# A two-layer block on one core: the token mixer in two parts, and layer 1's first mixer inside layer 0's last expert tile

## The chip, the cores and the metric

The kernel runs on one core of a Trainium2 chip, in fp32. The metric is the device time in microseconds (us) of one execution. The engines of the core work side by side and meet at semaphores: TensorE (PE: matrix products and transposes into PSUM), VectorE (DVE), ScalarE (ACT), GpSimd (POOL: here it issues the gathers) and SyncE (SP: here it issues the weight loads). Each engine goes through its own instructions strictly in order. All transfers share 16 DMA engines.

## The reference

Two layers act on 4 tiles of 128 latent tokens and 2 tiles of 128 context tokens, width 1024. Each layer has a token mixer and then a PEER expert layer, each followed by a residual and a layer norm:

```python
y, y_x = token_mixer(modulate(x, sh1, sc1), modulate(ctx, xsh1, xsc1), ...)
x = layer_norm(alpha * x + g1 * y, ln1_g[layer], ln1_b[layer])
f = peer(modulate(x, sh2, sc2), w_pq[layer], sub_keys[layer], u_tab[layer], v_tab[layer])
x = layer_norm(alpha * x + g2 * f, ...)      # and the same for ctx in layer 0
```

The mixer projects its input with w_in and forms three branches. Branch a is dense grouped attention with RMS norm and rope (8 heads, 2 key heads) over all 6 tiles; branch c is attention over a window of 128 tokens to either side, plus the context, with a sink; branch b is a convolution of three taps over the tokens, `gb * conv(gc * xb)`. Then `m = sum(sigmoid(gate_i) * (y_i @ w_branch[i]))` and `m @ w_out`. In layer 1 the context gives keys and values alone.

PEER picks for each token and each of 8 heads 16 of 16384 experts (product keys), gathers a row of u_tab and one of v_tab for each, 1024 wide, and returns `sum(gelu(x . u) * softmax * v)`.

## The kernel before

**Order.** `ORDER` names ten (layer, tile) units: 0 and 1 are layer 0's context tiles, 2 to 5 its latent tiles, 6 to 9 layer 1's latent tiles. Unit n is first mixed (mixer n) and then goes through its expert tile n. An expert tile has 128 slots. In slot S POOL issues one gather of u (128 partitions by 1024 fp32, one expert for each token) and one gather of v for 36 slots earlier (`BEHIND`); DVE forms the dot product of a u row (line 1463); PE sums two v rows in every second slot (`two_sums`), into banks 0 and 1 of PSUM. Both rings, ur and vr, hold 6 rows. A new u gather waits for the dot of the row six back, a v gather for the sum of the row six back. Every 16 slots a head is routed (top 16, on DVE), and PE makes the query product of a head three ahead, with two chunks of w_pq.

**The plan.** `plan()` (line 95) writes one list of steps, and all engines go through the same list. An entry is a slot (l, S) with the steps that it hosts, or steps alone. `hosted(n)` (line 123) says what expert tile n hosts:

- every tile n that is not the last of its layer hosts mixer n + 1, in 83 steps, one a slot from slot 0, and `turn` at slot 83. A mixer's step `mix(m, at)`: at 0 to 40 attention, eight pairs of heads, five slots a pair (scores, maxima, exponentials, transposes, copy; values and transposes of the pair before go in between), the dense branch first; 41 to 70 the merge, six groups (two halves of 512 columns by three branches) of four gate chunks and two branch chunks; 72 to 75 eight chunks of w_out; 76 to 82 residual and norm;
- tile 0 hosts beside that, from slot 87 and two a slot, the projections of both latent pairs of layer 0 (`proj` 1 and 2), their convolution over 512 columns (`conv` 1) and a row;
- tile 5, which hosts no mixer, has the 12 modulation pieces of layer 1 (48 chunks), five rows, the keys of the context (`proj` 3) and keys and queries of tiles 0 and 1 (`proj` 4).

Then layer 0 runs out: 36 slots of v rows, the end of tile 5 (`ends`), and then alone, with no slots beside it: `proj` 5 (keys and queries of tiles 2 and 3, which needs the new x of unit 5), `conv` 2 over 512 columns, mixer 6 in 83 steps, `turn`, and the lead (product, routing of the first heads). I call this stretch the seam. A similar stretch with mixer 0 opens the kernel.

**Data.** A `proj` job turns x tiles, modulates them into xTg (8 x 512 columns per partition), takes keys and values (`kT`, `vals`), queries, and spills turned x (xts), queries (qts) and convolution results (yts) to DRAM. A mixer loads its tile's qTt, xTt and ybt back. xTg and the mixer's buffers lie in one arena and overlap. hn, the input of the dot products, is made by `tile_begins` (lines 1453 and 1455) on DVE from x and two broadcast rows. Twenty such rows (`row`) are made by transposes and an ACT copy.

**Weights.** All weights come in chunks of 128 x 1024 fp32 (512 KB) over a ring of five, in the order of the plan (`load`, line 396); SP stops at the sixth until `w_used` says that the first was used. On line 399 stands

```python
w.wait_ge("w_used", c - NS + 1)
sp.dma_start(wring[:, c % NS, :], src).then_inc(w_in[c % NS], 16)
```

PE's hosted work uses banks 4 to 7; banks 0 to 3 belong to the experts.

Of the kernel before, what the change touches and what calls it, by code (L numbers as in the profile page):

```python
# [17 lines left out]
P = 128  # L18
D = 1024
# [5 lines left out]
HD = 64  # L25
# [45 lines left out]
def row_source(r):  # L71

    return {R_G1: (True, G1), R_S2: (True, SC2), R_H2: (True, SH2), R_G2: (True, G2),
            R_L1G: (False, 0), R_L1B: (False, 1), R_L2G: (False, 2), R_L2B: (False, 3)}[r]
# [3 lines left out]
ROWS = ([(r, 0, 1) for r in (R_G1, R_L1G, R_L1B, R_S2, R_H2, R_G2, R_L2G, R_L2B)]  # L78
        + [(R_G1, 0, 0), (R_S2, 0, 0), (R_H2, 0, 0), (R_G2, 0, 0)]
        + [(r, 1, 0) for r in (R_G1, R_L1G, R_L1B, R_S2, R_H2, R_G2, R_L2G, R_L2B)])  # L80


def rows_for_mix(m):
    return 8 if m < 2 else 9 if m < 6 else 17


def rows_for_h(n):
    return 8 if n < 2 else 11 if n < 6 else 17


def rows_for_end(n):
    return 8 if n < 2 else 12 if n < 6 else 20


def plan():


    out = []
    for e in range(4):
        out.append((None, [("mod", e, 0)]))  # L100
        if e:
            out.append((None, [("mod", e - 1, 1)]))
    out.append((None, [("mod", 3, 1)]))
    out += [(None, [("proj", 0, st)]) for st in range(18)]
    out += [(None, [("conv", 0, st)]) for st in range(16)]

    def begin(m, beside):
        for s in range(83):
            out.append((None, [("mix", m, s)] + beside.get(s, [])))
        out.append((None, [("turn", m)]))  # L110
        l = ORDER[m][0]
        for jj, st in ((0, 0), (0, 1), (0, 2), (1, 0), (0, 3), (1, 1), (1, 2), (0, 4), (2, 0), (1, 3), (2, 1), (2, 2), (1, 4)):
            out.append((None, [("lead", l, jj, st)]))

    beside = {}
    for e in range(4, MODS):
        beside.setdefault(4 * (e - 4) + 1, []).append(("mod", e, 0))
        beside.setdefault(4 * (e - 4) + 3, []).append(("mod", e, 1))
    for r in range(8):
        beside.setdefault(33 + r, []).append(("row", r))  # L120
    begin(0, beside)

    def hosted(n):
        at = {}
        if n + 1 < FIRST[ORDER[n][0]] + COUNT[ORDER[n][0]]:
            for s in range(83):
                at[s] = [("mix", n + 1, s)]
            at[83] = [("turn", n + 1)]
        if n == 0:
            steps = ([("proj", 1, st) for st in range(18)] + [("proj", 2, st) for st in range(18)]  # L130
                     + [("conv", 1, st) for st in range(16)] + [("row", 8)])
            for i, step in enumerate(steps):
                at.setdefault(87 + i // 2, []).append(step)
        elif n == 1:
            at[100], at[102] = [("row", 9)], [("row", 10)]
        elif n == 2:
            at[100] = [("row", 11)]
        elif n == 5:
            for e in range(MODS):
                at.setdefault(4 + 3 * e, []).append(("mod", MODS + e, 0))  # L140
                at.setdefault(6 + 3 * e, []).append(("mod", MODS + e, 1))
            for r in range(12, 17):
                at.setdefault(44 + 2 * (r - 12), []).append(("row", r))
            for i, st in enumerate((0, 1, 2, 3, 4, 5, 6, 7, 8, 9, 10)):
                at.setdefault(56 + i, []).append(("proj", 3, st))
            for st in range(18):
                at.setdefault(70 + 2 * st, []).append(("proj", 4, st))
        elif n == 6:
            at[100], at[102], at[104] = [("row", 17)], [("row", 18)], [("row", 19)]
        return at  # L150

    for l in range(LAYERS):
# [11 lines left out]
def chunk_counts(steps):  # L164

    used, n = {}, 0
    for at, beside in steps:
# [7 lines left out]
        for d in beside:  # L175
            if d[0] == "mod" and d[2] == 0:
                n += 4
            elif d[0] == "proj" and (2 <= d[2] < 6 or PAIRS[d[1]][3] and (6 <= d[2] < 10 or 11 <= d[2] < 15)):
                n += 1
            elif d[0] == "conv" and d[2] % 4 < 3:  # L180
                n += 1
            elif d[0] == "mix" and 41 <= d[2] < 71:
                n += len(CHUNKS_AT[(d[2] - 41) % 5])
# [35 lines left out]
def hybrid_dit_peer(nc, x, ctx, cc, w_mod, b_mod, w_qkv, q_norm, k_norm, conv_w, sink, w_conv, w_gb,  # L219
                    w_out, ln, w_pq, sub_keys, u_tab, v_tab, rope_c, rope_s, out):  # L220
    with ExitStack() as stack:
# [125 lines left out]
        def far_scores():  # L347

            return bank(5).rearrange("p (h n) -> p h n", h=2)
# [1357 lines left out]
```

## Time and profile before

| | before |
|---|---|
| median of 3 runs | 5172.78 us (5172.71 to 5173.66) |
| the profiled execution | 5177.72 us |
| its span | 5176.0 us |
| PE, DVE, POOL busy | 3824.4, 2791.6, 2779.3 us |
| moved by DMA | 1796.82 MB, mean 347 GB/s |
| granted clock of TensorE, mean | 0.86 |

The engines' names in the rows are as above; PEld is the weight load of TensorE, SPq a transfer's issue. `x8` counts instructions; an fp32 product with 512 columns counts as two. A row of a window has its stretch, its length, the busy times of PE, PEld, DVE, ACT and POOL with the count of instructions, then the granted clock, the DMA share and GB/s. The windows inside tiles begin and end at the dot product of a slot that 16 divides. The granted clock is a share of 2.4 GHz. The DMA share is the mean busy share of the 16 engines. Expert tiles n began (hn written) at 348.7 (0), 894.7, 1316.6, 1738.9, 2166.6, 2582.3 (5), 3487.7 (6), 3915.0, 4341.5 and 4761.1 us (9).

### The profile page before, as it was taken

To read this page: it belongs to the slowest core of one execution; us is meant where nothing else is said; L and a number is where in the kernel's file an instruction comes from. 1 tells how busy PE (TensorE), PEld (TensorE's weight loads), DVE (VectorE), ACT (ScalarE), POOL (GpSimd) and SP (SyncE) were. 2 spreads that over 40 slices of the span, in tenths; PEclk is the share of its full clock that TensorE was granted. 3 is DMA by queue.
4 is the path that set the end of the run, shared out by engine and by line. 5 is a ranking of instruction groups with operands and counts; after the bars stand their busy time and mean duration, and the time that the engine had idled before them with its cause. 6 is when DMAs were issued, how large, how long until landed. Compare 5 with 4: busy or idle time off the path is not lost.

```text
span 5176.0 us, 47460 instructions
## 1 busy us (share of the span) xinstructions
PE 3824.4 (74%) x15312; PEld 1709.4 (33%) x15312; DVE 2791.6 (54%) x7071; ACT 866.8 (17%) x1954; POOL 2779.3 (54%) x2575
## 2 busy tenths in 40 slices
PE   7767788885886787688666759587867866876555
PEld 4543333431432342243223214445323323421111
DVE  1156454746755665675645622126467556656662
ACT  1211111311311221131101100213112212210100
POOL 0026523756756765775755640004567557657775
PEclk9878899998998898899778989586989988998787
DMA  6679976999999999999999972066999999999998
GB/s 209 220 265 369 402 261 241 372 409 408 391 388 408 391 379 406 395 384 409 407 409 392 404 282 87 33 245 211 408 406 384 382 410 399 381 409 407 399 408 314
DMA packets 509655, 1796.82 MB, mean 347 GB/s; under 512 B 56288, under 2 KB 71904, under 8 KB 509152
## 3 DMA queue, kind: packets, MB, share of 16 engines
q0 software_dynamic: 368640, 1342.34, 66.8%
q1 hardware_dynamic: 122336, 438.34, 22.2%
q10 hardware_dynamic: 18432, 13.11, 0.8%
q8 instruction: 123, 2.02, 0.2%
q14 instruction: 124, 1.02, 0.1%
HBM read 1778.36 MB, written 15.20 MB: 347 GB/s over the span
## 4 chain that ended last, share of the span: by engine, by line
DMA 38%; PE 36%; issue 10%; POOL 7%; DVE 6%; ACT 2%; SPq 0%; POOLq 0%; DVEq 0%
PE ps L568 33%; DMA vr<-in_v_tab,idxT 30%; DMA ur<-in_u_tab,idx 5%; POOL ur L530 4%; POOL vr L541 3%; PE ps L571 3%; DMA wring<-in_w_mod 2%; DVE ur L1463 1%; DVE mx L1357 1%; ACT arena L1064 1%; DVE mx L1355 1%; ACT arena L983 1%; ACT arena L1067 0%; DMA wring<-in_w_out 0%; DVE ps L1352 0%
## 5 line engine op out<-in xcount | busy, mean ns | idle before, releaser
L568 PE MATMUL ps<-vr,spread 128*32 128x512 f32 x5120 | 1526.0, 727 | 975.1 <-DMA vr<-in_v_tab,idxT 926.8
L1463 DVE CUSTOM_DVE_ANT_0 ur<-ur,hn 128x1024 f32<-128x1024 f32 x1280 | 1564.3, 1222 | 1183.2 <-DMA ur<-in_u_tab,idx 1180.3
L530 POOL DMA_INDIRECT ur<-in_u_tab,idx x1280 | 1383.3, 1081 | 1273.2 <-DVE idx L1546 742.9
L541 POOL DMA_INDIRECT vr<-in_v_tab,idxT x1280 | 1392.3, 1088 | 1103.6 <-PE ps L568 492.4
L568 PE MATMUL ps<-wring,arena 128*128 128x512 f32 x2272 | 1042.0, 607 | 13.6 <-ACT arena L983 9.4
L568 PEld LDWEIGHTS ps<-vr,spread 128*32 128x32 f32 x5120 | 312.1, 122 | 1869.4 <-issue 1865.4
L568 PEld LDWEIGHTS ps<-wring,arena 128*128 128x128 f32 x2272 | 426.0, 194 | 550.7 <-issue 522.9
L568 PE MATMUL ps<-wring,hT 128*128 128x256 f32 x1280 | 339.5, 413 | 7.4 <-ACT hT L983 6.0
L571 PE MATMUL ps<-ident,arena 128*128 128x128 f32 x1000 | 188.2, 334 | 188.1 <-DVE arena L1381 103.2
L568 PEld LDWEIGHTS ps<-wring,hT 128*128 128x128 f32 x1280 | 251.1, 206 | 157.2 <-issue 115.5
L571 PEld LDWEIGHTS ps<-ident,arena 128*128 128x128 f32 x1000 | 144.5, 170 | 282.5 <-DVE arena L1381 140.7
L568 PE MATMUL ps<-vals,arena 128*128 128x64 f32 x1472 | 208.6, 304 | 22.7 <-ACT arena L1082 17.4
L568 PEld LDWEIGHTS ps<-vals,arena 128*128 128x128 f32 x1472 | 201.5, 219 | 54.4 <-ACT arena L1082 32.6
L568 PE MATMUL ps<-arena,wring 128*128 128x512 f32 (+1 forms) x576 | 212.4, 531 | 3.8 <-issue 3.8
L1108 ACT COPY q_sb<-ps 128x256 f32<-128x256 f32 x80 | 29.8, 373 | 952.4 <-PE ps L568 952.4
L568 PE MATMUL ps<-kT,arena 64*128 64x256 f32 (+2 forms) x576 | 144.2, 557 | 13.4 <-DMA arena<-qts 13.4
L568 PEld LDWEIGHTS ps<-arena,wring 128*128 128x128 f32 x576 | 111.7, 195 | 101.9 <-issue 96.3
L1064 ACT ACTIVATE arena<-ps,nm 128x512 f32<-128x512 f32 (+2 forms) x160 | 91.7, 573 | 221.9 <-DVE nm L1368 221.9
L568 PE MATMUL ps<-wring,csilu 128*32 128x128 f32 x1536 | 80.3, 350 | 53.2 <-DMA wring<-in_w_mod 53.0
L1355 DVE TENSOR_REDUCE mx<-ps 128x2 f32<-128x512 f32 x64 | 43.8, 684 | 139.0 <-PE ps L568 139.0
L1089 ACT ACTIVATE arena<-ps 128x512 f32<-128x512 f32 x60 | 35.8, 597 | 487.4 <-PE ps L568 487.0
L1463 DVE DVE_READ_ACCUMULATOR2_ANT dots<- 128x1 f32 x1280 | 105.8, 83 | 0.0
(158 smaller groups left out, 2686.3 us busy)
## 6 DMA issues: line engine op xcount, KB each, us to landing
wring<-in_w_gb SPq DMA_DIRECT2D x360, 512.0 KB, 7.8
wring<-in_w_pq SPq DMA_DIRECT2D x160, 512.0 KB, 8.0
wring<-in_w_mod SPq DMA_DIRECT2D x96, 512.0 KB, 7.2
wring<-in_w_out SPq DMA_DIRECT2D x80, 512.0 KB, 7.6
wring<-in_w_qkv SPq DMA_DIRECT2D x64, 512.0 KB, 6.7
ur<-in_u_tab,idx POOLq DMA_INDIRECT x1280, 8.2
vr<-in_v_tab,idxT POOLq DMA_INDIRECT x1280, 8.3
wring<-in_w_conv SPq DMA_DIRECT2D x36, 512.0 KB, 3.6
```

The costliest lines, as they stand in the source:

```text
L530: nc.gpsimd.indirect_dma_start(ur[:, row % UR, :], None, u_rows, bass.IndirectOffsetOnAxis(ap=idx[:, at:at + 1], axis=0)).then_inc(u_in[ro ...
L541: nc.gpsimd.indirect_dma_start(vr[:, row % VR, :], None, v_rows, bass.IndirectOffsetOnAxis(ap=idxT[:, pair % 3, i:i + 1], axis=0)).then_in ...
L568: return nc.tensor.matmul(o, lhsT, rhs, start=first, stop=last, skip_group_check=True)
L571: return nc.tensor.transpose(o, src, ident[:])
L983: m = nc.scalar.activation(o[:, k, :], bank(b + k // 4, k % 4 * P, (k % 4 + 1) * P), ACT.Identity, scale=mod_t[:, l, KD * scale + k, kind: ...
L1064: k = nc.scalar.activation(pr[:, hd, 0:n], bank(4 + 2 * hd, 0, n), ACT.Exp, bias=bias, scale=SCALE, accum_out=sums[:, a % 2, 0, hd:hd + 1])
L1089: nc.scalar.activation(sg, bank(4 + 2 * (e6 % 2)), ACT.Sigmoid).then_inc(s["sg_done"], 1)
L1108: nc.scalar.copy(flat(q_sb), bank(2, 0, 2 * P)).then_inc(s["q_copied"], 1)
L1355: ch.inc(v.tensor_reduce(mx[:, a % 2, 1, :], far_scores(), AX, ALU.max))
L1357: ch.inc(v.tensor_reduce(top2, near_scores(0, n), AX, ALU.max))
L1463: v.tensor_tensor_reduce(u, u, hn[:], 1.0, 0.0, ALU.mult, ALU.add, dots[:, j % 2, k:k + 1]).then_inc(s["dots_done"], 1)
```

## The change

The single numbered jobs are split into small steps, and the plan puts groups of them into slots. In particular:

- `proj` becomes keys jobs (two tiles or one; the last, LATE, is tile 3 of layer 1 alone) and queries jobs (two tiles). Queries and convolutions of tiles 2 and 3 are moved into a later expert tile; xTg is read back from xts for them. A convolution job now covers two tiles with one column of overlap (258 columns), five jobs in place of three.
- A mixer is two parts: windowed attention, then the merge of the convolution branch, of the windowed branch and of the dense branch's gates; then dense attention, then the merge of the dense branch (`merge_last`), w_out, norm. For mixer 6 the first part is hosted in tile 5, and the second stands alone after the last tile's keys, with two dense pairs in work at a time: the second in PSUM banks 0 to 3 and in the u buffers.
- The modulation pieces of layer 1 move from tile 5 to tile 4. The rows R_S2 and R_H2 go (20 rows become 14); hn is now made by PE, which turns hT back at slot 127 of the tile before, and a DVE copy.
- A mixer's loads on SP wait until every chunk issued so far was used, and for all spills so far.

```diff
+KEYS = [(0, (4, 5)), (0, (0, 1)), (0, (2, 3)), (1, (4, 5)), (1, (0, 1)), (1, (2,)), (1, (3,))]
+LATE = 6
+QUERIES = [(0, 4, False), (0, 0, False), (0, 2, True), (1, 0, False), (1, 2, True)]
+CONVS = [(0, 4, 0, 256, 0), (0, 0, 0, 258, 0), (0, 2, 254, 258, 2), (1, 0, 0, 258, 0), (1, 2, 254, 258, 2)]
+BRANCHES = (1, 2, 0)
+GROUP_CHUNKS = ((0, 1, 2, 3, 4, 5), (0, 1, 2, 3, 4, 5), (0, 1, 2, 3)) * 2 + ((4, 5), (4, 5))
...
+def keys_job(j):
+    tiles = KEYS[j][1]
+    return ([[("xt", j, i)] for i in range(len(tiles))] + [[("kvp", j, part)] for part in range(4)] + [[("kvv", j)]]
+            + [[("kvr", j, i)] for i in range(len(tiles))] + [[("kvt", j)]])
+def queries_job(j):
+    return ([[("qx", j)]] + [[("qp", j, 0, part)] for part in range(4)] + [[("qs", j), ("qp", j, 1, 0)]]
+            + [[("qr", j, 0, 0), ("qp", j, 1, 1)], [("qr", j, 0, 1), ("qp", j, 1, 2)], [("qp", j, 1, 3)], [("qt", j, 0)]]
+            + [[("qr", j, 1, 0)], [("qr", j, 1, 1)], [("qt", j, 1)]])
+def attention(m, br):
+    qs = range(4) if br else range(4, 8)
+    out = [[] for _ in range(24)]
+    for i, q in enumerate(qs):
+        for off, kind in enumerate(("sc", "mx", "ex", "tp", "ev", "va", "yn", "ty", "yc")):
+            out[5 * i + off].append((kind, m, q))
+    return out
+def attention_alone(m):
+    order = ("sc4 sc5 mx4 ex4 mx5 ex5 tp4 ev4 sc6 mx6 va4 yn4 tp5 ev5 ex6 ty4 yc4 sc7 mx7 va5 yn5 tp6 ev6 ex7 ty5 yc5 "
+             "va6 yn6 tp7 ev7 ty6 yc6 va7 yn7 ty7 yc7").split()
...
+def merge_last(m):
+    out = [[("gp", m, 6, 4)], [("gp", m, 6, 5)], [("gp", m, 7, 4), ("ml", m, 6)], [("gp", m, 7, 5)], [("mt", m, 0), ("ml", m, 7)]]
+    out += [[("wo", m, 0)], [("wo", m, 1)], [("mt", m, 1), ("wo", m, 2)]] + [[("wo", m, k)] for k in range(3, KD)]
+    return out + [[("on", m, st)] for st in range(7)]
...
+    def mixer(m):
+        return [[("in", m)]] + attention(m, 1) + merge_first(m) + attention(m, 0) + merge_last(m)
...
+        if n == 0:
+            put(mixer(1), 0, 73)
+            put([[("turn", 1)], [("row", 6)]], 74, 76)
+            put(keys_job(1) + keys_job(2), 76, 104)
+            put(queries_job(1), 104, 126)
+        elif n == 1:
+            put(conv_job(1), 0, 18)
+            put(mixer(2), 18, 85)
+            put([[("turn", 2)]], 85, 86)
+            put(queries_job(2) + conv_job(2), 87, 126)
+        elif n in (2, 3, 7, 8):
+            put(mixer(n + 1), 0, 84)
+            put([[("turn", n + 1)]], 84, 85)
+            if n == 2:
+                put([[("row", 7)]], 100, 101)
+        elif n == 4:
+            put(mixer(5), 0, 78)
+            put([[("turn", 5)]], 78, 79)
+            put([[("mod", MODS + e, 0)] + ([("mod", MODS + e - 1, 1)] if e else []) for e in range(MODS)]
+                + [[("mod", 2 * MODS - 1, 1)]], 80, 126)
+        elif n == 5:
+            put([[("row", 8)], [("row", 9)], [("row", 10)]] + keys_job(3) + keys_job(4), 0, 28)
+            put(queries_job(3), 28, 42)
+            put(keys_job(5), 43, 53)
+            put(conv_job(3), 53, 72)
+            put([[("in", SPLIT)]] + attention(SPLIT, 1) + merge_first(SPLIT), 72, 128)
+        elif n == 6:
+            put(mixer(7), 0, 84)
+            put([[("turn", 7)]], 84, 85)
+            put([[("row", 11)], [("row", 12)], [("row", 13)]] + queries_job(4) + conv_job(4), 86, 126)
         if n + 1 < FIRST[ORDER[n][0]] + COUNT[ORDER[n][0]]:
+            put([[("hn", n + 1)]], 127, 128)
...
         if l == 0:
-            out += [(None, [("proj", 5, st)]) for st in range(18)]
-            out += [(None, [("conv", 2, st)]) for st in range(16)]
-            begin(6, {})
+            alone(keys_job(LATE) + attention_alone(SPLIT) + merge_last(SPLIT))
+            lead(SPLIT)
...
+                elif kind == "in":
+                    if c["kv"]:
+                        w.wait_ge("w_used", ring[0])
+                    for k in range(c["kv"]):
+                        if kept(k):
+                            w.wait_ge(f"xsp{k}", 16 * len(KEYS[k][1]))
+                    for k in range(c["q"]):
+                        w.wait_ge(f"qsp{k}", 32)
+                    for k in range(c["cv"]):
+                        w.wait_ge(f"ysp{k}", 64)
+                    w.wait_ge("y_read", c["out"])
...
+            def turn_back(n):
+                free_banks(("hn", n))
+                w.wait_ge("hT_done", n + 1)
+                for k in range(KD):
+                    m = turn(bank(4 + k // 4, k % 4 * P, (k % 4 + 1) * P), hT[:, k, :])
+                m.then_inc(s["hn_mm"], 1)
...
             def tile_begins(n):
-                ch.inc(v.tensor_tensor(hn[:], xt, rows[:, R_S2, :], ALU.mult))
-                ch.wait()
-                v.tensor_tensor(hn[:], hn[:], rows[:, R_H2, :], ALU.add).then_inc(s["hn_done"], 1)
+                w.wait_ge("hn_mm", n + 1)
+                v.tensor_copy(hn[:], ps[:, 4 * BW:6 * BW]).then_inc(s["hn_done"], 1)
```

`put(groups, lo, hi)` spreads the groups evenly over the slots lo to hi. `free_banks(d)` lets PE wait, at the first product of a job, until all jobs that the plan has before it have left their banks.

## Rows read from the trace of the kernel before

**Rows 1.** Page, 40 slices: busy share of the DMA engines, tenths
```profile
DMA  6679976999999999999999972066999999999998
```

**Rows 2.** Windows by stage: us, busy per engine, clock, DMA share, GB/s
```profile
349.00:895.00 546.00, 435.20 (x1376) 194.35 (x1378) 299.49 (x751) 87.98 (x194) 246.96 (x220) 0.87 0.85 315
...
895.00:1317.00 422.00, 319.79 (x1274) 137.62 (x1272) 265.51 (x681) 83.72 (x189) 279.53 (x258) 0.89 1.01 397
...
1739.00:2167.00 428.00, 323.85 (x1282) 138.81 (x1280) 268.30 (x686) 84.34 (x187) 278.89 (x258) 0.88 1.00 391
...
2582.00:3016.00 434.00, 293.28 (x1690) 117.56 (x1690) 241.40 (x592) 56.60 (x114) 267.31 (x253) 0.83 1.02 402
...
3078.00:3242.00 164.00, 136.77 (x326) 62.63 (x324) 42.59 (x75) 13.30 (x29) 0.00 (x0) 0.89 0.27 84
...
3242.00:3366.00 124.00, 78.06 (x310) 61.58 (x311) 21.10 (x59) 30.00 (x95) 0.00 (x0) 0.53 0.07 27
...
3366.00:3447.00 81.00, 79.39 (x188) 35.11 (x187) 7.18 (x11) 7.58 (x11) 0.00 (x0) 0.97 0.79 275
...
3447.00:3488.00 41.00, 22.82 (x90) 16.86 (x90) 25.00 (x87) 8.30 (x23) 5.62 (x6) 0.75 0.54 194
...
3488.00:3915.00 427.00, 307.93 (x1130) 152.01 (x1132) 257.99 (x669) 80.91 (x183) 246.12 (x220) 0.81 0.90 346
...
4761.00:5099.00 338.00, 198.04 (x686) 56.21 (x683) 217.37 (x523) 27.20 (x50) 256.92 (x253) 0.79 1.02 404
```

**Rows 3.** Windows inside tile 0 (two) and tile 5 (one), 16 slots each
```profile
381.00:415.00 34.00, 18.13 (x73) 13.28 (x73) 31.45 (x94) 11.65 (x33) 22.68 (x18) 0.60 0.87 291
...
689.00:848.00 159.00, 149.06 (x420) 65.88 (x421) 59.93 (x138) 19.61 (x39) 32.39 (x33) 0.95 0.65 213
...
2647.00:2717.00 70.00, 40.93 (x413) 18.95 (x407) 27.31 (x76) 4.04 (x11) 35.57 (x32) 0.74 1.03 409
```

**Rows 4.** TensorE's timeline, seam: start, us, what [idle before <-releaser]
```profile
3086.37 1.94 PE L571 MATMUL ps<-ident,x_all 128*128 128x128 f32 x8 [8.23 <-DVE x_all L1595]
...
3096.26 30.06 PE L568 MATMUL ps<-wring,arena 128*128 128x512 f32 x64 [2.99 <-ACT arena L983]
...
3150.08 85.37 PE L568 MATMUL ps<-arena,wring 128*128 128x512 f32 x192 [1.15 <-issue]
...
3242.69 3.36 PE L568 MATMUL ps<-kT,arena 64*128 64x512 f32 x8 [7.23 <-DMA arena<-qts]
...
3260.61 3.37 PE L568 MATMUL ps<-kT,arena 64*128 64x512 f32 x8
...
3268.81 2.82 PE L571 MATMUL ps<-ident,arena 128*128 128x128 f32 x12 [1.33 <-ACT arena L1067]
...
3273.22 3.74 PE L568 MATMUL ps<-vals,arena 128*128 128x64 f32 x24 [1.59 <-ACT arena L1082]
...
3311.14 2.51 PE L568 MATMUL ps<-kT,arena 64*128 64x256 f32 x8
...
3460.14 6.70 PE L568 MATMUL ps<-wring,hT 128*128 128x256 f32 x16 [2.99 <-ACT hT L983]
```

**Rows 5.** Timeline of all engines: a key chain's ends, and hn of tile 6
```profile
3112.63 0.65 ACT L1008 COPY vals<-ps 128x256 f32<-128x256 f32 x2 [16.42 <-PE ps L568]
...
3119.16 0.42 DVE L1231 TENSOR_TENSOR arena<-ps,arena 128x256 f32<-128x256 f32 x1
...
3487.65 1.22 DVE L1453 TENSOR_TENSOR hn<-x_all,rows 128x1024 f32<-128x1024 f32 x1
```

**Rows 6.** Window over the first 48 slots of tile 2
```profile
1319.00:1466.00 147.00, 124.64 (x652) 66.72 (x649) 112.71 (x298) 47.86 (x124) 109.14 (x96) 0.93 0.97 374
```

**Rows 7.** Timeline of TensorE: one query chunk in tile 2
```profile
1341.56 1.89 PE L568 MATMUL ps<-wring,hT 128*128 128x256 f32 x8
```

**Rows 8.** DMA issues: count, KB each, median us from issue to landing
```profile
arena<-qts SPq DMA_DIRECT2D x10, 512.0 KB, 6.9
...
ur<-in_u_tab,idx POOLq DMA_INDIRECT x1280, 8.2
```

More of the change, by code:

```diff
@@ L99, in plan @@
     for e in range(4):
-        out.append((None, [("mod", e, 0)]))
+        alone([[("mod", e, 0)]])
         if e:
[L102 to L111, printed above, removed]
+            alone([[("mod", e - 1, 1)]])
@@ L116, in plan @@
+    groups = mixer(0)
     for e in range(4, MODS):
[L117 to L121, printed above, removed]
+        groups[4 * (e - 4) + 1].append(("mod", e, 0))
+        groups[4 * (e - 4) + 3].append(("mod", e, 1))
+    for r in range(EARLY_ROWS):
+        groups[40 + 2 * r].append(("row", r))
+    alone(groups)
@@ L123, in hosted @@
+    lead(0)
     def hosted(n):
         at = {}
-        if n + 1 < FIRST[ORDER[n][0]] + COUNT[ORDER[n][0]]:
[L126 to L149, printed above, removed]
@@ new lines, in values @@
+            def values(m, q):
+                a = 8 * m + q
+                br, _, at = pair_of(m, q)
+                near, far = keys_of(m, br)
+                tiles = near + far
+                w.wait_ge("pts_done", a + 1)
+                w.wait_ge("yT_done", a - (1 if two_at_a_time(m, q) else 0))
+                for half in range(2):
+                    for b, kt in enumerate(tiles):
+                        k = mm(bank(7 - 4 * at, half * HD, (half + 1) * HD), pts[at][:, half, b, :],
+                               vals[:, br, kt, half * HD:(half + 1) * HD], b == 0, b == len(tiles) - 1)
+                k.then_inc(s["pv_mm"], 1)
@@ L1035, in conv, with turned @@
-            def conv(g, st):
-                l, t0, nt = GROUPS[g]
+            def turned(j, i):
+                l, tiles = KEYS[j]
+                w.wait_ge("tx_mm", XT_BEFORE[j] + i + 1)
+                for before in range(j):
+                    if kept(before):
+                        w.wait_ge(f"xsp{before}", 16 * len(KEYS[before][1]))
+                o = columns(j, i)
+                modulate(o, 4, l, int(tiles[i] >= LAT), SH1, SC1).then_inc(s["xT_done"], 1)
+                if kept(j):
+                    act.wait_ge(s["xT_done"], XT_BEFORE[j] + i + 1)
+                    nc.scalar.dma_start(xts[l, tiles[i]], o).then_inc(s[f"xsp{j}"], 16)
@@ new lines, in values_out @@
+            def values_out(j):
+                w.wait_ge("w_used", USED["kvp", j, 3])
+                tiles = KEYS[j][1]
+                n = len(tiles)
+                for i in range(n):
+                    m = nc.scalar.copy(vals[:, :, tiles[i], :], bank(6 + i, 2 * P, BW).rearrange("p (a b) -> p a b", b=P))
+                m.then_inc(s["v_copied"], 1)
+                w.wait_ge("ksq_done", j + 1)
+                nc.scalar.activation(kss[:, 0:n, :], kss[:, 0:n, :], ACT.Sqrt).then_inc(s["ksd_done"], 1)
```

1212 lines of the change are left out of this document (614 added, 598 removed).

## The prediction

> **What bounds the kernel now.** I read the slices of the page first [rows 1]: the DMA engines stand at 9 tenths or more in 29 of 40 slices; the holes are the first slices, 6 and 7, and 24 to 28. Then the windows by stage [rows 2]. A slot below is one of the 128 steps of an expert tile. Each window of an expert tile runs from one tile's hn to the next. Tiles 1 to 5, 7 and 8 have a DMA share of 1.00 to 1.02 at 391 (tile 3) to 402 GB/s (tile 5); 1, 3 and 5 are shown. They take as long as their bytes, 415 to 434 us. Tile 9, which hosts nothing, takes 338. Three stages are not DMA bound. Tile 0 takes 546 us at 315 GB/s, and most of that excess is in one stretch [rows 3]: 16 slots take 159 us there, TensorE is busy 149 of them. The seam between the layers (3078 to 3488) takes 410 us at 27 to 275 GB/s, with POOL idle. Tile 6 has 346 GB/s, as its first 36 slots have no v gathers beside them. Last I followed the seam on TensorE [rows 4]: transposes and keys and queries of the last two tiles, a convolution over 512 columns (192 instructions, 85.37 us), attention, merge, norm, lead.
>
> So the question is what the seam loses, and what the hosting tiles pay.
>
> **The seam.** What stays in it after 3078, where its last v sum ends:
> - Norm of x, 8.2 us (the idle before the transposes), then one tile's transposes and modulation, 1.94 + 2.99: 13.1 us, against 18.2 before for two tiles [rows 4].
> - Four key chunks for one tile. 64 instructions took 30.06 us [rows 4], so 16 take 7.5. The key chain that lay under the query product is now bare: on two tiles it ran from the v copy at 3112.63 to the rope's end at 3119.58 [rows 5], 7.0 us; I take 5 for one, plus 1.3 for transposes and copy: 13.8.
> - Four dense pairs of heads. Alone they took 68 us, from the first scores at 3242.69 to those of the next branch at 3311.14 [rows 4], 17.1 each. Of the pair shown TensorE worked 3.37 (scores) + 0.47 (y, estimated from one of eight at the lower clock) + 2.82 (transposes) + 3.74 (values) = 10.4 us; the rest is waiting for maxima and exponentials. With two pairs in two sets of banks the work of one covers the waits of the other. Walking the written order with these durations (the first two pairs' scores, maxima and exponentials to 8.4; 11 to 12 for each later pair; the last one's waits bare) I get 54 us. Ends: 34 (TensorE's share halved, were it at the upper clock) and 68 (no overlap).
> - Four branch chunks and eight of the out projection, 16 and 32 instructions at 0.44 (85.37 / 192 [rows 4]), 21; products with the gates, adds and row transposes between, 2.6 by similar rows: 23.6.
> - Norm, transposes, modulation up to the first query as at the seam's start, 13.1. Then hT is turned back for hn, 8 transposes, 2.0 by the 1.94 of such a row. Lead 27.5 as before (3460.14 [rows 4] to hn at 3487.65 [rows 5]).
>
> Sum 13.1 + 13.8 + 54 + 23.6 + 13.1 + 2.0 + 27.5 = 147 us against 410: **-262 us**, ends -285 and -235.
>
> A rule weighs here. The granted clock of the attention window of the seam was 0.53, near the 1.2 GHz level, while the merge after it ran at 0.97 [rows 2]; TensorE worked there in bursts of 3 to 4 us with waits of 1.3 and 1.6 between them [rows 4]. The Trainium skill (TensorE: Matmul & The Clock Gate, "HAM oscillation — how this bites in real kernels") says that short bursts with idle gaps bring the array back to the lower clock each time. The trace agrees with that for one pair at a time. By the page, closing the gaps with a second pair could release the clock; the attention would then come to the 34 us end above. I keep the lower level, since waits are left in the walk.
>
> **What tiles pay.** In a DMA-bound tile 1 MB more costs 2.5 us (402 GB/s), a chunk (0.524 MB) 1.3 us.
> - *Tile 0*: 80 hosted chunks become 60, less spill of queries and yts: 172 MB (315 x 546) to 159. At 400 GB/s that is 399; slots 16 to 31 ran at 291 GB/s for 34 us [rows 3], the 16 before them much the same, so 64 us with 18 lost; 8 for stalls. 425, **-121** (ends -146 and -86: key steps sit 1.4 slots apart).
> - *Tile 1*: gets both convolutions of layer 0 (24 chunks), the late queries (8) and the reload of three xts tiles. 167.5 MB becomes 189: 470 us by bytes. TensorE: 320 busy now [rows 2], plus 2 x 46 for the convolutions (192 instructions each, 8 of 256 columns in 1.89 us [rows 7]), 32 for queries, 4 for rows and hn: 448. In a mixer's first 48 slots, which hold its eight pairs, it idled 22 of 147 us [rows 6], and 102 of 422 in all. The mixer is also squeezed from 83 slots into 67, a pair every 3.3 slots. I take 510, **+88** (ends +48 and +140).
> - *Tiles 2, 3, 7, 8*: same bytes. A pair comes every 4.2 slots rather than 5; eight pairs took about 122 us (40 of the 48 slots in 147 us [rows 6]), 15.2 each; 4.2 slots would take 11 at tile 9's 2.64 us a slot (338 / 128). The chain, not the slot, sets this, and attention now drains twice: **+4 each, +16** (ends -10, +60).
> - *Tile 4*: takes over 48 modulation chunks, 25.2 MB: +63, and +4 as above: **+67** (ends +60, +90). These chunks already ran at 409 GB/s in tile 5 [rows 3].
> - *Tile 5*: 64 chunks before (48 + 4 + 12), 64 after (12 keys, 8 queries, 12 convolution, 32 merge). Bytes no change. New: SP waits before the mixer's loads until every issued chunk is used and the last spill of the convolution has landed; behind it stand the merge's weights, and TensorE waits for q. A q load took 6.9 us to land [rows 8]; with the spill ahead and two slots between, 8 net. The convolution needs 46 us of TensorE in 19 slots: 9 over bytes. Two chained stretches: 9. **+26** (ends 0, +66).
> - *Tile 6*: 20 chunks, reload and spills, 14 MB: 35, and 5 of stalls: **+40** (ends +30, +70).
> - *hn*: VectorE no longer makes hn with two passes (1.22 each [rows 5]) but copies out of PSUM, 1.2 as one such pass, after TensorE has done the last two-row sum (1.9) and 8 transposes (2.0). That v row is issued behind the last u row on POOL, so the first dot comes some 4 us later. Five u rows are in flight meanwhile and landing takes 8.2 us [rows 8], so I charge 1 us in 8 tiles: **+8** (ends -5, +30).
> - *Prologue*: two rows fewer, one hn more, attention in two parts; **-2**.
>
> Sum: -262 - 121 + 88 + 16 + 67 + 26 + 40 + 8 - 2 = **-140 us**. The profiled execution took 5177.7 us (span 5176.0), so 5038; the median of the runs is 4.9 us lower: **5033 us**.
>
> Cross-check by idle DMA time. Added are 24 convolution chunks, 4 of keys and 6 reloads, 34 x 0.524 = 17.8 MB, 44 us. The seam's 410 us carried 47 MB (its four windows [rows 2]), 118 us at 402, so 292 idle; after it carries 13 MB in 147 us, 115 idle. Tile 0 had 116 idle and keeps 26. That is 44 - 177 - 90 = -223 with no new stall anywhere, the most there is: 4950.
>
> **Rivals.**
> 1. *Everything hides* (0.09): the tiles run at 400 GB/s also with the new work, and most of the 80 us between the two sums is not there: 4965 with 15 left, 4950 with none. For it: TensorE has room, 320 of 422. Against: it works in order and idles in each attention chain.
> 2. *Half is given back* (0.20): tiles 0, 1 and 6, with keys, queries and convolution at a step per 1.1 to 1.4 slots, come near their upper ends together (35 + 52 + 30 of 117): 5105 to 5160. Tile 0 before is its evidence: 16 slots in 159 us with two steps a slot [rows 3]. Against: half the columns and half the density now.
> 3. *Slower* (0.06): the period of a hosted pair. If putting its steps into 4.2 slots makes each pair slower, since TensorE stands in the chain while v gathers wait (a ring of six), sixty pairs in tiles 1 to 8 pay. From 15.2 us a pair, 140/60 = 2.3 more, so 17.5, wipes the gain out; at 19 (the seam's 17.1 with one two-row sum of 1.9 between) it is +228 - 140 = +88: 5261. Against it: hosted pairs ran at 0.93 of the clock, not 0.53 [rows 2, 6].
> 4. *The seam doesn't shrink as written* (0.02 of its own, no change in all): TensorE's waits for all earlier stages, or the bare key chain, would have to cost 140 more than the 147: 5173.
>
> **How the numbers follow.** The forecast has 0.63: its own range by adding the ends as independent, about 70 either way. The range 4960 to 5115 takes that in, with part of rivals 1 and 2. Differences under 0.2% (10 us) can't be told from none here. Faster 0.90, same 0.03, slower 0.07.
>
> **What would show it.** From the last v sum of layer 0 to hn of tile 6: 147 us, the dense attention 54 of it, two sets of scores back to back. Tile 0 near 425, tile 1 near 510 with TensorE busy about 450, tile 4 near 483 at 400 GB/s, tile 5 near 460, tile 6 near 467, tiles 2 and 3 within 10 of before. It is wrong if the seam is over 200, or if the DMA share of tiles 2, 3, 7, 8 falls clearly under 0.98.

## The result, and the profile after

| | before | after | ratio, 95% interval |
|---|---|---|---|
| median | 5173.22 us | 4993.77 us | 0.9645, 0.9623 to 0.9667 |
| span of the profiled execution | 5176.0 | 4985.6 | |

The kernel is 3.6% faster, 179 us at the medians and 190 in the profiled spans. Forecast were 140 and 5033 us; the range 4960 to 5115 holds the time.

The windows by stage of the changed kernel, to be read against [rows 2]; they run from one tile's hn to the next. The row of 61 us is the run-out of layer 0's v rows, the row of 145 us the seam, and the last one tile 6:

```profile
0.00:370.00 370.00, 278.81 (x1554) 169.04 (x1554) 68.04 (x195) 56.56 (x139) 9.56 (x21) 0.85 0.58 205
370.00:784.00 414.00, 324.33 (x1128) 138.21 (x1128) 268.76 (x702) 82.40 (x187) 253.06 (x225) 0.90 1.01 394
784.00:1281.00 497.00, 421.85 (x1728) 221.87 (x1728) 293.32 (x750) 87.29 (x197) 284.94 (x252) 0.92 0.97 371
1281.00:1714.00 433.00, 329.53 (x1296) 141.25 (x1296) 266.44 (x683) 84.02 (x186) 282.80 (x261) 0.88 1.01 393
...
2143.00:2625.00 482.00, 352.92 (x2046) 162.83 (x2047) 264.26 (x693) 84.35 (x197) 284.14 (x255) 0.88 1.01 399
2625.00:3076.00 451.00, 363.37 (x1368) 161.69 (x1366) 260.96 (x647) 75.52 (x172) 275.07 (x251) 0.92 1.00 387
3076.00:3137.00 61.00, 40.08 (x152) 9.53 (x148) 1.59 (x5) 3.38 (x4) 29.95 (x32) 0.89 0.88 313
3137.00:3282.00 145.00, 95.53 (x354) 63.52 (x352) 50.05 (x140) 31.96 (x83) 5.62 (x6) 0.75 0.27 94
3282.00:3726.00 444.00, 366.25 (x1432) 192.10 (x1432) 279.47 (x718) 87.99 (x193) 253.40 (x222) 0.89 0.95 365
```

The seam fell from 410 to 145 us. Tile 0 went from 315 to 394 GB/s: it is now bound by its bytes like the others, and 132 us shorter. Tile 4 still moves 399 GB/s and is 66 us longer, which is what 48 chunks cost. Of the expert tiles only tile 1 (0.97, with TensorE busy 422 of 497 us) and tile 6 (0.95) have a DMA share below 1.00. The profile's page says the same of the whole; against [rows 1] only slices 1 to 3 and 26 to 27 are still holes:

```profile
DMA  5749999999999999999999999359999999999998
```

By stages, from the first dot of one tile to the first dot of the next (the seam: from the end of the last v sum to the first dot):

| stage | before | after | difference | forecast |
|---|---|---|---|---|
| up to the first dot | 351.2 | 370.1 | +19 | -2 |
| tile 0 | 546.0 | 414.1 | -132 | -121 |
| tile 1 | 421.9 | 496.6 | +75 | +88 |
| tiles 2, 3, 7, 8 | 1696.0 | 1715.2 | +19 | +16 |
| tile 4 | 415.7 | 481.5 | +66 | +67 |
| tile 5 with the run-out | 493.3 | 515.2 | +22 | +26 |
| seam | 412.0 | 142.3 | -270 | -262 |
| tile 6 | 427.4 | 443.3 | +16 | +40 |
| tile 9 and the end | 412.4 | 407.4 | -5 | 0 |
| hn (in the tiles above) | | | | +8 |

The seam on TensorE, changed kernel, to be read against [rows 4]:

```profile
3148.09 1.97 PE L686 MATMUL ps<-ident,x_all 128*128 128x128 f32 x8 [8.14 <-DVE x_all L1741]
3153.05 9.78 PE L683 MATMUL ps<-wring,arena 128*128 128x512 f32 x16 [2.99 <-ACT arena L1099]
3167.07 0.69 PE L686 MATMUL ps<-ident,arena 128*128 128x128 f32 x2 [4.25 <-DVE arena L1381]
3168.22 5.29 PE L683 MATMUL ps<-kT,arena 64*128 64x512 f32 x16 [0.46 <-ACT kT L1131]
...
3189.37 2.77 PE L686 MATMUL ps<-ident,ur 128*128 128x128 f32 x12
3191.93 0.42 PE L686 MATMUL ps<-ident,arena 128*128 128x128 f32 x1
3193.72 1.89 PE L683 MATMUL ps<-kT,arena 64*128 64x512 f32 x8 [1.38 <-ACT ur L1204]
3195.55 2.89 PE L683 MATMUL ps<-vals,ur 128*128 128x64 f32 x24
...
3216.26 8.90 PE L683 MATMUL ps<-wring,arena 128*128 128x512 f32 x16 [0.35 <-ACT arena L1210]
3253.98 1.97 PE L686 MATMUL ps<-ident,hT 128*128 128x128 f32 x8 [2.99 <-ACT hT L1099]
```

Two pairs' scores stand together as `x16`; from there to the end of the last y transposes, 3168.22 to 3215.91, it is 47.7 us where the walk gave 54 and one pair at a time took 68 in the kernel before. The bare key chain is the 4.25 us of idle before 3167.07. Part of the reason for 47.7 rather than 54 is the clock: scores took 5.29 for the first two pairs and 1.89 for the last, where the walk had 3.37 each. The window over the stretch has the granted clock at 0.64 and TensorE busy for 38.4 us, where the walk had 41.6. The waits are the other half, 9.3 us against 12.4 (54 less 41.6).

```profile
3168.00:3216.00 48.00, 38.44 (x180) 31.71 (x180) 10.96 (x28) 17.12 (x46) 0.00 (x0) 0.64 0.00 1
```

### The profile page after: what moved, and what is told of

It is laid out like the page before. It is cut to its first block, busy times and chain, and to the rows that moved or that the text cites. A ratio compares the mean times of both kernels' runs of the same rounds, so it can differ in the third digit from the quotient of the medians.

```text
span 4985.6 us, 48540 instructions
## 1 busy us (share of the span) xinstructions
PE 3777.8 (76%) x15728; PEld 1743.7 (35%) x15728; DVE 2774.0 (56%) x7108; ACT 867.4 (17%) x1963; POOL 2799.3 (56%) x2575
## 2 busy tenths in 40 slices
DMA packets 519164, 1814.71 MB, mean 364 GB/s; under 512 B 56961, under 2 KB 77697, under 8 KB 518657
## 4 chain that ended last, share of the span: by engine, by line
PE 38%; DMA 37%; issue 9%; DVE 7%; POOL 6%; ACT 3%; SPq 1%; POOLq 0%; ACTq 0%; DVEq 0%
PE ps L683 34%; DMA vr<-in_v_tab,idxT 27%; DMA ur<-in_u_tab,idx 5%; POOL ur L645 3%; PE ps L686 3%; POOL vr L656 3%; DMA wring<-in_w_gb 2%; DVE ur L1609 1%; DMA wring<-in_w_mod 1%; ACT arena L1187 1%; DVE mx L1500 1%; DMA wring<-in_w_pq 1%; ACT arena L1099 1%; ACT arena L1190 1%; DMA wring<-in_w_qkv 1%
## 5 line engine op out<-in xcount | busy, mean ns | idle before, releaser
L683 PE MATMUL ps<-vr,spread 128*32 128x512 f32 x5120 | 1477.1, 705 | 764.7 <-DMA vr<-in_v_tab,idxT 728.6
L645 POOL DMA_INDIRECT ur<-in_u_tab,idx x1280 | 1399.7, 1093 | 1020.4 <-DVE idx L1692 494.6
L683 PE MATMUL ps<-wring,arena 128*128 128x512 f32 x2272 | 1078.5, 619 | 51.4 <-DMA wring<-in_w_gb 21.5
L683 PE MATMUL ps<-wring,hT 128*128 128x256 f32 x1280 | 323.8, 398 | 22.2 <-DMA wring<-in_w_pq 22.2
L683 PE MATMUL ps<-arena,wring 128*128 128x258 f32 (+1 forms) x960 | 218.1, 385 | 4.8 <-ACT arena L1151 3.5
L683 PEld LDWEIGHTS ps<-vals,arena 128*128 128x128 f32 x1424 | 185.5, 211 | 58.3 <-ACT arena L1204 33.8
L683 PEld LDWEIGHTS ps<-arena,wring 128*128 128x128 f32 x960 | 181.3, 191 | 44.3 <-issue 13.4
L683 PE MATMUL ps<-kT,arena 64*128 64x256 f32 (+2 forms) x576 | 144.3, 558 | 53.1 <-DMA arena<-qts 36.5
L1526 DVE TENSOR_TENSOR arena<-ps,rec 128x128 f32<-128x128 f32 x80 | 23.3, 292 | 202.8 <-PE ps L683 202.2
L1187 ACT ACTIVATE arena<-ps,nm 128x256 f32<-128x256 f32 (+2 forms) x156 | 88.8, 570 | 218.0 <-DVE nm L1511 218.0
L683 PEld LDWEIGHTS ps<-kT,arena 64*128 64x128 f32 x576 | 79.2, 220 | 98.4 <-issue 47.0
```

The lines of the kernel that those rows point to most:

```text
L645: nc.gpsimd.indirect_dma_start(ur[:, row % UR, :], None, u_rows, bass.IndirectOffsetOnAxis(ap=idx[:, at:at + 1], axis=0)).then_inc(u_in[ro ...
L683: return nc.tensor.matmul(o, lhsT, rhs, start=first, stop=last, skip_group_check=True)
L1187: k = nc.scalar.activation(pr[at][:, hd, 0:n], bank(b + 2 * hd, 0, n), ACT.Exp, bias=bias, scale=SCALE, accum_out=sums[:, a % 2, 0, hd:hd ...
L1526: v.tensor_tensor(ysb[:, a % 2, :].rearrange("p (h f) -> p h f", f=HD), bank(7 - 4 * at, 0, P).rearrange("p (h f) -> p h f", f=HD), over(r ...
```

## The experiments

They ran in three groups, and in each the kernel before took longer than above: 5329 us in the first group (mixer 6 not split, one pair at a time, steps spread, hT at slot 125 for the first time), 5354 and 5353 in the other two. So a whole time is compared inside its group, by its ratio to the kernel before. The first group had no run of the changed kernel; for stages I take it from the others. Four experiments were executed once each (mixer 6 not split, one pair at a time, steps spread, attention first), and they are read by their stages. A stage that an edit doesn't touch still differs by 5 to 10 us between runs, so a single pair of stages shows no less than that.

**Mixer 6 not split.**

```diff
-            put([[("in", SPLIT)]] + attention(SPLIT, 1) + merge_first(SPLIT), 72, 128)
...
-            alone(keys_job(LATE) + attention_alone(SPLIT) + merge_last(SPLIT))
+            alone(keys_job(LATE) + [[("in", SPLIT)]] + attention(SPLIT, 1) + merge_first(SPLIT)
+                  + attention_alone(SPLIT) + merge_last(SPLIT))
```

> Mixer 6 is not split: tile 5 hosts keys, queries and convolution only, and windowed attention and the first merge of mixer 6 stand alone in the seam. Theory A (a hosting tile pays for bytes): tile 5 gets shorter by 32 chunks at 1.3 us, 42, and by some 10 us of waits for the mixer's loads, 50 in all; the seam gets longer by four windowed pairs at 13.8 us, 55, by 32 chunks at 4 x 0.44 us, 56, and a load of about 8: 118. Sum +68 against the changed kernel, about 5055 profiled. Rival B (tile 5 has TensorE time to spare and hosts the part nearly for nothing): tile 5 shorter by under 15, sum over +100. Rival C (most of the seam's gain came from the moved convolution and queries, the split is worth little): sum under +30.

Tile 5 with its hosted work gone, and the seam:

```profile
2664.00:3078.00 414.00, 305.68 (x1104) 125.80 (x1104) 247.10 (x609) 54.94 (x112) 274.41 (x250) 0.85 0.98 378
3141.00:3393.00 252.00, 179.93 (x610) 110.44 (x605) 64.94 (x178) 52.37 (x143) 5.64 (x6) 0.76 0.36 128
```

The seam is 251 us from the last v sum to the first dot, 109 more than the changed kernel's 142 (expected 118). From first to last dot tile 5 takes 415 us against 461 and 468 in the two runs of the same group that hosted the part: 46 to 53 less (expected 50). So hosting pays some 50 us for 109. The whole took 5172 us, 0.9706 of before, against 0.9586 and 0.9598 for the changed kernel: 1.1% or about 60 us, where theory A expected 68, rival B over 100 and rival C under 30. Theory A holds. Convolution and queries moved out, keys of one tile, and the dense pairs two at a time brought the seam from 412 to 251, some 160 of the 270 us; the split brought the rest. Of the 160, only the pairs were tested by themselves, in the next experiment.

**One pair at a time in the seam.**

```diff
-            alone(keys_job(LATE) + attention_alone(SPLIT) + merge_last(SPLIT))
+            alone(keys_job(LATE) + attention(SPLIT, 0) + merge_last(SPLIT))
```

> The four dense pairs in the seam one after the other instead of two at a time. Theory (the second pair covers the waits of the first): the stretch from the first dense scores to the end, 48 us in the changed kernel, goes back to 68 or a little less, +18 to +20, granted clock back from 0.66 towards 0.53. Rival (TensorE's own work at the lower clock sets it): under +6.

Its timeline on TensorE, one pair and the next pair's scores:

```profile
3233.04 3.21 PE L683 MATMUL ps<-kT,arena 64*128 64x512 f32 x8
3236.18 0.33 PE L686 MATMUL ps<-ident,arena 128*128 128x128 f32 x1
3241.08 2.82 PE L686 MATMUL ps<-ident,ur 128*128 128x128 f32 x12 [4.57 <-ACT ur L1190]
3245.49 5.38 PE L683 MATMUL ps<-vals,ur 128*128 128x64 f32 x24 [1.59 <-ACT ur L1204]
3250.80 3.37 PE L683 MATMUL ps<-kT,arena 64*128 64x512 f32 x8
```

The window over the four pairs, to be read against that of 48 us above:

```profile
3215.00:3286.00 71.00, 45.46 (x181) 35.84 (x182) 11.45 (x28) 17.45 (x45) 0.00 (x0) 0.55 0.00 0
```

A pair takes 17.8 us, with waits of 4.57 and 1.59. The seam from last v sum to first dot is 166 us against 142, +24, a little over the +18 to +20 expected. From the first scores to the last y transpose it is 70.4 us against 47.7, 22.7 more. Of these 7 are TensorE's own work (45.5 us busy against 38.4, at a granted clock of 0.55 against 0.64) and the other 16 are waits. So the second pair gains twice: it fills waits, and for part of the time the products run at the upper clock. The rival, under 6 us, is out.

**Tile 0's steps spread, in the kernel before.**

```diff
-                at.setdefault(87 + i // 2, []).append(step)
+                at.setdefault(87 + i * 39 // 53, []).append(step)
```

> The kernel before, with the 53 steps that tile 0 hosts after its mixer (projections, convolution over 512 columns, a row) over slots 87 to 126 instead of 87 to 113. Theory A (TensorE's work was the limit there: 149 of 159 us busy): tile 0 shorter by some 15 to 25 us only, because 13 more slots of gathers lie beside the same work, 546 to about 525. Rival B (two steps a slot, each waiting for another engine, made the stall): shorter by 60 or more.

The hosted steps now lie over both windows (the first dot of slot 80 to that of 96, and from there to the end):

```profile
683.00:776.00 93.00, 78.29 (x261) 34.43 (x259) 53.99 (x131) 16.30 (x33) 33.07 (x31) 0.93 0.84 299
776.00:885.00 109.00, 104.91 (x290) 45.12 (x292) 40.79 (x91) 7.21 (x13) 27.54 (x27) 0.97 0.60 197
```

Tile 0 is 8 us shorter than in [rows 2], in a run whose tile 1 is 12 longer for a reason that lies outside the edit. The gain is 8 us as measured and about 20 if tile 0 was slowed as tile 1 was. The changed kernel's tile 0 took 0 to 6 us more in these groups than above, so the truth is more likely near 10: under theory A's 15 to 25, and far from the 60 of rival B. TensorE is busy 105 of 109 us in the second window, as it was 149 of 159 in [rows 3]. So the density of the steps was not the matter. That it was the amount of products is argued from these busy times: the changed kernel, which has the convolution elsewhere, keeps TensorE busy 324 us in tile 0 against 435.

**hT turned back at slot 125.**

```diff
-            put([[("hn", n + 1)]], 127, 128)
+            put([[("hn", n + 1)]], 125, 126)
```

> hT is turned back for hn at slot 125 instead of slot 127. In the changed kernel the first dot of a tile came 8 to 9 us after the last dot before it in tiles 1, 3, 4, 8 (4.1 before the change). Theory A (the wait for TensorE's last two-row sum is exposed and costs DMA time): that gap falls to 3 to 4 us in all tiles, and the time by 3 us in each of 5 tiles, 10 to 20 in all. Rival B (the DMA queues stay full through the gap, as the prediction had it with 1 us a tile): the gap falls but the time by under 6.

> hT turned back at slot 125, now beside the changed kernel on one chip. The gap before a tile's first dot, summed over the eight tile starts within a layer, was 52 us in the changed kernel and 35 with this edit. Theory A (exposed): 10 to 17 us less time. Rival B (hidden by the gathers in flight): under 5.

What it was to cure is this, in the changed kernel at the start of tile 4 (the last dot of tile 3, TensorE's last two-row sum, the transposes, the copy, the next dot):

```profile
2134.49 1.23 DVE L1609 CUSTOM_DVE_ANT_0 ur<-ur,hn 128x1024 f32<-128x1024 f32 x1 [3.08 <-DMA ur<-in_u_tab,idx]
2137.15 3.63 PE L683 MATMUL ps<-vr,spread 128*32 128x512 f32 x8 [5.44 <-DMA vr<-in_v_tab,idxT]
2140.71 1.33 PE L686 MATMUL ps<-ident,hT 128*128 128x128 f32 x8
2142.07 1.22 DVE L1601 COPY hn<-ps 128x1024 f32<-128x1024 f32 x1 [5.93 <-PE ps L686]
2143.33 1.23 DVE L1609 CUSTOM_DVE_ANT_0 ur<-ur,hn 128x1024 f32<-128x1024 f32 x1
```

The gap between two dots is 8.8 us here. With the edit the eight gaps summed to 35 us in the first group and 32 in the other instead of 52, as expected, but the time did not follow. Beside the changed kernel the ratios were 0.9597 (0.9575 to 0.9619) with the edit and 0.9598 (0.9573 to 0.9622) without, in the first group 0.9588 with it. That favours rival B, but each interval is some 12 us to either side, so 10 us can't be ruled out by this pair. Nor is it shown that the gathers in flight bridge the gap: tile 5 with the run-out took 531 to 543 us in the four runs with this edit and 521 to 533 in six without it, for a cause that stays open, and that alone may hide a gain.

**The modulation pieces under the second attention of mixer 0, the rows beside the out projection.**

```diff
-        groups[4 * (e - 4) + 1].append(("mod", e, 0))
-        groups[4 * (e - 4) + 3].append(("mod", e, 1))
+        g = 4 * (e - 4) + 1 if e < 8 else 57 + 5 * (e - 8)
+        groups[g].append(("mod", e, 0))
+        groups[g + 2].append(("mod", e, 1))
...
-        groups[40 + 2 * r].append(("row", r))
+        groups[82 + 2 * r].append(("row", r))
```

> Prologue only: of the eight modulation pieces beside mixer 0 four are moved under its second attention, and the six rows beside the out projection. The changed kernel reaches its first dot at 370.1 us, 18.9 later than before: 7.4 are there when the convolution starts (the bared key chain), 12 appear between there and the end of mixer 0. Theory A (the second attention, 28 us with nothing beside it, is time that the modulation filled before): first dot 8 to 14 us earlier. Rival B (the weights' transfers, not TensorE, set the first part): under 3 us, since the same bytes come.

The changed kernel's second attention, and the same place with the edit:

```profile
278.25 1.97 PE L683 MATMUL ps<-vals,arena 128*128 128x64 f32 x8 [0.68 <-ACT arena L1202]
280.14 1.23 PE L683 MATMUL ps<-kT,arena 64*128 64x256 f32 x4
281.30 0.47 PE L686 MATMUL ps<-ident,arena 128*128 128x128 f32 x1
283.42 1.11 PE L686 MATMUL ps<-ident,arena 128*128 128x128 f32 x4 [1.65 <-ACT arena L1187]
```

```profile
267.01 0.70 PE L684 MATMUL ps<-kT,arena 64*128 64x256 f32 x4
267.64 1.95 PE L684 MATMUL ps<-wring,csilu 128*32 128x128 f32 x64
269.52 0.33 PE L687 MATMUL ps<-ident,arena 128*128 128x128 f32 x1
269.98 0.33 PE L687 MATMUL ps<-ident,msb 128*128 128x128 f32 x1
270.90 0.66 PE L687 MATMUL ps<-ident,arena 128*128 128x128 f32 x4 [0.59 <-ACT arena L1188]
```

The first dot came at 357.6 us instead of 371.9 in the same group: 14 less, the upper end of theory A. In all runs it came at 354 to 360 us with this edit (three) and at 365 to 376 without it and without q's own place (eight), 11 less at the means. The 64 modulation products fill the wait that stood bare. The ratio is 0.9556 (0.9529 to 0.9584) against 0.9586; by itself the whole run can't tell 14 us from noise, the stage can.

**q's own place.** The mixer's buffers are laid out anew, so that qTt lies where neither projection nor convolution writes. Its load no longer waits for the last issued chunk to be used or for the convolution's spill, only for the spills of queries and turned x and for the scores of the mixer before.

```diff
-        qTt = region(0, 2, BC, P)
-        xTt = region(4, KD, P)
+        qTt = region(31, 2, BC, P)
+        xTt = region(6, KD, P)
...
-                    if c["kv"]:
-                        w.wait_ge("w_used", ring[0])
                     for k in range(c["kv"]):
                         if kept(k):
...
                     for k in range(c["q"]):
                         w.wait_ge(f"qsp{k}", 32)
+                    w.wait_ge("s_mm", 8 * m)
+                    sp.dma_start(qTt.rearrange("p a b c -> p (a b c)"), qts[l, t]).then_inc(s["q_in"], 16)
+                    if c["kv"]:
+                        w.wait_ge("w_used", ring[0])
                     for k in range(c["cv"]):
                         w.wait_ge(f"ysp{k}", 64)
                     w.wait_ge("y_read", c["out"])
-                    sp.dma_start(qTt.rearrange("p a b c -> p (a b c)"), qts[l, t]).then_inc(s["q_in"], 16)
```

> q's buffer is moved to a part of the arena that no projection or convolution uses, and its load no longer waits for the last used chunk and the convolution's spill. In the changed kernel TensorE stood 8.97 us for it in tile 1, in mixer 2's first slot. Theory A (these waits stop the v ring and cost DMA time): tile 1 shorter by 6 to 9 us, tile 5 by about as much, others by nothing; 10 to 18 us in all. Rival B (the transfers queue up meanwhile, and the time comes back in the DMA-bound slots behind): under 5.

The place in tile 1 where TensorE stood, first in the changed kernel and then with the edit:

```profile
847.07 1.91 PE L683 MATMUL ps<-vr,spread 128*32 128x512 f32 x8
857.95 2.50 PE L683 MATMUL ps<-kT,arena 64*128 64x256 f32 x8 [8.97 <-DMA arena<-qts]
```

```profile
842.62 1.91 PE L684 MATMUL ps<-vr,spread 128*32 128x512 f32 x8
844.46 1.47 PE L684 MATMUL ps<-kT,arena 64*128 64x256 f32 x8
```

Tile 1 was not the only such place. TensorE waited for q five times in the changed kernel, 36.5 us in all, where the kernel before has two such waits of 13.4 together. Besides the 6.21 in the prologue and the 8.97 in tile 1 these are, at the mixers' starts in tiles 2, 5 and 7:

```profile
1283.79 2.50 PE L683 MATMUL ps<-kT,arena 64*128 64x384 f32 x7 [5.51 <-DMA arena<-qts]
2892.73 2.50 PE L683 MATMUL ps<-kT,arena 64*128 64x256 f32 x8 [8.85 <-DMA arena<-qts]
3730.95 2.91 PE L683 MATMUL ps<-kT,arena 64*128 64x384 f32 x8 [7.00 <-DMA arena<-qts]
```

With the edit none of the five is left. Yet the tiles hardly followed. Tile 1 took 489.9 us against 502.8, more than the 9 us of the wait, but 501.2 and 494.5 in the two runs that hold all three edits, against 497 to 506 in nine without. Tile 5 with the seam showed nothing (666.9 and 664.2), nor did tile 2 (457.0 and 457.2) and tile 7 (453.8 and 455.3), against theory A. The ratio is 0.9563 (0.9544 to 0.9583) against 0.9586 (0.9566 to 0.9606), 0.2% and inside the two intervals. So a gain of some 10 us is likely but not shown, and most of the 37 us of waits cost no time.

**All three edits.**

> hn at slot 125, the modulation pieces spread, and q's own buffer together. They touch different places, so their gains should add: 10 to 14 (prologue) + 10 to 18 (q) + 10 to 17 (hn), 30 to 49 us under the changed kernel. If the DMA queues hide hn's gap and q's wait: 12 to 18 only.

> hn early, modulation pieces spread, q's own buffer, beside the changed kernel: if hn's gap is hidden, 0.4 to 0.6% under it (prologue 14, q about 12); if it is exposed, 0.7% or more.

Ratios 0.9534 (0.9515 to 0.9553) and 0.9538 (0.9519 to 0.9557), against 0.9586 and 0.9598 for the changed kernel in its two groups:

> The changed kernel itself, as the base for the others on the same chip. Ratio to the kernel before 0.962 to 0.968 as measured already, whatever the chip's pace of gathers.

> The changed kernel once more, as the base for the three others, which run beside it. Ratio to before 0.958 to 0.967.

That is 5107.8 us against 5133.65 in the last group, and 5106.0 against 5131.9 in the other: 26 us or 0.5 to 0.6% better than the changed kernel, with intervals that don't meet. The first expectation had 12 to 18 us if hn's gap and q's wait are hidden and 30 to 49 if neither is; 26 lies between. The medians of the single edits were 11 (modulation) and 16 us (q) under the changed kernel, which leaves nothing for hn. By stages only the prologue's 12 us shows in both runs. This version beats both kernels.

The changed kernel's own ratio was 0.9586 in its first group here, under the 0.962 to 0.968 that was expected: where everything takes 3% longer, the change brings 4.1% rather than 3.6.

**Attention first in tiles 0 and 6.**

```diff
+        if m in (1, 7):
+            return [[("in", m)]] + attention(m, 1) + attention(m, 0) + merge_first(m) + merge_last(m)
         return [[("in", m)]] + attention(m, 1) + merge_first(m) + attention(m, 0) + merge_last(m)
```

with the waits for merges and attention exchanged to fit.

> In tiles 0 and 6 only (mixers 1 and 7) both attention parts run before the merges, as before the change. Question: why tile 6 paid 16 us where 40 was forecast. Theory A: in these two tiles the first 36 slots have no v gathers; with the mixer in two parts its 32 merge chunks begin at slot 20 and fill transfer time that stood idle while attention came first. Then tile 6 gets longer by 10 to 20 us (its slot 80 comes at about 290 rather than 276 us) and tile 0 by 5 to 15. Rival B (TensorE simply had more spare time in slots 86 to 126 than assumed): both within 4 us of the changed kernel.

Slots 16 to 47 of tile 6, first with attention first, then the changed kernel in the same group:

```profile
3420.00:3528.00 108.00, 80.05 (x351) 52.49 (x351) 69.18 (x189) 33.23 (x79) 56.92 (x48) 0.75 0.73 254
```

```profile
3403.00:3516.00 113.00, 90.58 (x265) 39.90 (x267) 62.53 (x165) 24.20 (x43) 56.45 (x48) 0.91 0.92 359
```

The times are much alike, but the second moved 359 GB/s against 254: 41 MB against 27, merge chunks that the first still has to fetch. Slot 80 came 299 us after the tile's first dot instead of 279. Tile 6 took 467.2 us against 445.2, tile 0 427.7 against 414.3. That is theory A, in tile 6 slightly over its upper end of 20. The whole took 5179 us, 45 more than the changed kernel; 35 of them are in these two tiles.

## Why the prediction was right, and where its sizes were off

- *The seam, -262 forecast, -270 measured.* Its parts came as written, each but the attention within 1.5 us: 13.1 us to the first product, 15.2 for keys and key chain (13.8 forecast), 24.9 for the merge and out projection (23.6), 13.2 for norm and transposes, 26.5 for the lead (27.5). The attention was 47.7 us and not 54; one pair at a time costs 23 us more. On the clock I had kept the lower level (1.2 GHz); the trace shows both levels in the stretch, a grant of 0.64 with two pairs together against 0.55 with one. The Trainium skill (TensorE: Matmul & The Clock Gate, "HAM oscillation — how this bites in real kernels") says that when an idle gap behind a burst of products is long enough, the next burst starts at the lower clock. The trace agrees in part: with waits of 4.57 us the grant was 0.55, with waits of at most 2.98 it was 0.64, and not the upper level throughout.
- *Tile 0, -121 / -132.* What rival 2 built on, steps close together, was not the cause: spreading them brought 8 to 20 us of the 132. The explanation by the amount of TensorE's work (convolution over 512 columns) is supported by the busy times. The 11 us beyond the forecast have a cause that the sum left out: the 18 us lost in the first slots were kept in full, while attention in two parts brings weights there, and attention first costs 13 us in this tile.
- *Tile 1, +88 / +75.* TensorE was busy 422 us, not 448, and the tile moved 184 MB (371 x 497), not 189. The q wait was priced in tile 5 alone, where it came as forecast (8.85 for 8). It stood here as well, at 8.97, and in tiles 2 and 7; that it costs a tile its full length is not borne out by the runs with q's own place.
- *Tile 4, +67 / +66.* Bytes at 2.5 us a MB. *Tile 5, +26 / +22.* Here the bytes stayed, 174 MB before and after, and most of the 22 us are stalls as forecast: the q wait, and a DMA share of 0.92 in slots 32 to 47, where TensorE is busy 59 of 69 us. How the 22 divide among the forecast's three stalls wasn't tested.
- *Tile 6, +40 / +16: this term was mis-sized.* "Bytes at 2.5 us, plus stalls" assumed that the mixer costs there what it did. The two-part order puts the merge's weights into slots that have no v gathers beside them, where the DMA engines stood idle. Going back to attention first makes tile 6 22 us longer, which is nearly the whole miss of 24.
- *Prologue, -2 / +19: mis-sized, with the other sign.* "Attention in two parts" hid both causes: the key chain, bare here too (7.4 us when the convolution starts), and the second attention, no longer over the modulation products. The edit that refills it brings 11 to 14 back; I had worked out this bare chain in the seam and not asked where else the same job runs alone.
- *hn, +8.* The gap came as described, 5.6 to 9 us in six of eight starts, but no cost of it could be measured; 0 fits better than 8, within the some 10 us that the runs leave open.
- *Tiles 2, 3, 7, 8, +16 / +19.* No tile is more than 11 us longer, so the slower pairs of rival 3 had no part. Their 19 us weren't looked into by an experiment.

The errors of +21, of -24, -13, -11, -8, -8, -5 and -4, and of +3 and -1 sum to -50 us, the 190 of the spans against 140 forecast. At the medians 5033 was 39 us high; the result lies between the forecast and rival 1, whose 4965 left 15 us for stalls. The stalls of tile 1 stayed. That the sum fits better than its terms is in part luck: the prologue's +21 and tile 6's -24 cancel, and nearly all the other errors have one sign. The cross-check's added bytes came out exactly: 17.9 MB more, 1814.71 against 1796.82, where it had 17.8. One sum of the prediction is off. The listed ends, added as independent, give about 66 us to the faster side but about 100 to the slower, not 70 either way, so by its own terms the upper bound of 5115 was low.

## What to carry to other kernels

When stages are bound by bytes, price moved work by its bytes at the rate of the tile that takes it in, and its old place by the time that it took there; here 48 chunks cost 66 us, and half a mixer cost its host 50 us and saved 109 in the seam. Ask of every chain that loses its cover (keys without queries beside them, attention without modulation) in all the places where the job runs. A host's slots aren't alike: those that lack one of the usual transfers took weights more cheaply (22 and 13 us in two tiles), so put the weight-heavy part there. And a wait that an edit removes, as the 37 us for q, isn't time that it saves: look whether the stage got shorter.

## What was not expected of the hardware

The same kernel took 3% more where the experiments ran, with nothing of its own changed: in the changed kernel tile 9, which hosts nothing, took 369 us from its first dot to its last, against 333 in the profiled execution above. The median distance of two dots was about the same (2.59 and 2.56 us), but single ones reached 6 to 13 us, as if single gathers landed late; the cause was not found. The changed kernel's ratio to the kernel before moved by 0.6%, which is more than the intervals allow for. Stage times of one run can't be set against those of another group to better than some per cent.
